# Last expert pair's down weights by quarters of output columns, scattered outputs added on VectorE, and a new order in heads and gates

## The reference

```python
  x   = LN(x)
  A   = (rms_norm(HGRN2(q, f, i, state)) * silu(g_o)) @ w_o_a      # 8 heads, 128 x 128 state each
  B   = silu(LN(depthwise_conv31(u_a * sigmoid(u_b)))) @ w_o_b
  mix = (sigmoid(gate_a) * A + sigmoid(gate_b) * B) @ w_out
  x   = LN(alpha * x + mix)
  x   = LN(alpha * x + MoE(x))   # 16 experts in 4 groups: best group, then top-2 in it
```

## Time and profile before

| what | us |
|---|---|
| median of 3 runs (lowest, highest) | 912.35 (911.97, 913.24) |
| the profiled execution: its own time | 911.96 |
| the profiled execution: its span | 910.1 |
| PE busy in the span | 848.2 |
| DVE busy in the span | 397.4 |

### The profile page before, as it was taken

The page is one execution under the profiler, slowest core; times in us unless marked ns, Lnnn a source line. Parts: engine busy times, 40 slices in busy tenths (PEclk is TensorE's granted clock), DMA queues, the critical chain, the costliest instruction groups (busy, mean ns, idle before and its releaser), DMA issues.

```text
span 910.1 us, 12810 instructions
## 1 busy us (share of the span) xinstructions
PE 848.2 (93%) x4904; PEld 532.4 (58%) x4904; DVE 397.4 (44%) x720; ACT 227.5 (25%) x358; POOL 108.1 (12%) x173
## 2 busy tenths in 40 slices
PE   4999999999999999999999999999999899898983
PEld 3989888898989866546554353535435244252330
DVE  6787788879999823215310313103031040310205
ACT  6566666653356131003010011000100001000001
POOL 1366667620000000000000000000000000000000
PEclk9999999999999999998999999999999999999997
DMA  8222222524436523905499999999999999999951
GB/s 302 71 79 80 78 78 85 188 80 154 171 104 237 212 107 153 372 0 208 163 429 428 428 428 428 426 428 427 429 427 429 428 428 428 428 428 428 427 255 59
DMA packets 30420, 248.95 MB, mean 274 GB/s; under 512 B 4462, under 2 KB 7918, under 8 KB 17962
## 3 DMA queue, kind: packets, MB, share of 16 engines
q1 hardware_dynamic: 27840, 247.07, 66.2%
q10 hardware_dynamic: 2538, 1.32, 0.5%
HBM read 245.89 MB, written 2.48 MB: 273 GB/s over the span
## 4 chain that ended last, share of the span: by engine, by line
PE 53%; DVE 19%; DMA 15%; POOL 5%; issue 4%; ACT 3%; POOLq 0%; DVEq 0%; ACTq 0%; SPq 0%
PE ps L437 52%; DMA ring<-in_w_up_e 8%; DMA ring<-in_w_gate_e 7%; DVE ar L1503 6%; DVE split_t L1511 3%; POOL ring L1240 2%; DVE ring L1390 1%; DVE ring L1403 1%; POOL ring L1226 1%; PE ps L772 1%; DVE split_w L1349 1%; POOL ar L1255 0%; DVE mid L1521 0%; POOL ar L1253 0%; DVE split_w L1354 0%
## 5 line engine op out<-in xcount | busy, mean ns | idle before, releaser
L437 PE MATMUL ps<-ring,ar 128*64 128x512 f32 (+1 forms) x1120 | 268.2, 594 | 10.6 <-DMA ring<-in_w_gate_e 3.9
L437 PEld LDWEIGHTS ps<-ring,ar 128*64 128x64 f32 (+1 forms) x1120 | 99.1, 140 | 168.5 <-issue 152.6
L437 PE MATMUL ps<-ring,xT 128*64 128x512 f32 (+2 forms) x896 | 161.4, 458 | 7.0 <-DMA ring<-in_w_gate_e 6.7
L437 PEld LDWEIGHTS ps<-ring,xT 128*64 128x64 f32 (+1 forms) x896 | 84.3, 152 | 79.0 <-issue 63.8
L1720 DVE TENSOR_TENSOR ar<-ar,ps 128x512 f32<-128x512 f32 (+1 forms) x42 | 28.7, 684 | 224.4 <-PE ps L437 224.4
L437 PE MATMUL ps<-split_x,split_t 128*128 128x320 f32 x672 | 101.7, 313 | 4.7 <-DVE split_t L1511 4.1
L437 PEld LDWEIGHTS ps<-split_x,split_t 128*128 128x128 f32 x672 | 100.1, 191 | 6.0 <-issue 3.8
L437 PE MATMUL ps<-split_x,split_w 128*128 128x320 f32 x480 | 80.4, 324 | 6.6 <-DVE split_w L1354 2.7
L437 PEld LDWEIGHTS ps<-split_x,split_w 128*128 128x128 f32 x480 | 73.8, 195 | 11.1 <-issue 2.5
L437 PE MATMUL ps<-ar 128*64 128x64 f32 (+6 forms) x304 | 74.1, 375 | 3.1 <-ACT ar L1174 1.2
L1503 DVE SCALAR_TENSOR_TENSOR ar<-ar,params 128x350 f32<-128x350 f32 x116 | 67.7, 584 | 4.1
(11 more groups left out here) (190 smaller groups left out, 721.8 us busy)
## 6 DMA issues: line engine op xcount, KB each, us to landing
ring<-in_w_gate_e SPq DMA_DIRECT2D x32, 2048.0 KB, 27.5
ring<-in_w_up_e SPq DMA_DIRECT2D x32, 2048.0 KB, 25.9
ring<-in_w_down_e SPq DMA_DIRECT2D x32, 2048.0 KB, 31.7
ring<-in_w_in SPq DMA_DIRECT2D x56, 512.0 KB, 4.3
ring<-in_w_o_a SPq DMA_DIRECT2D x8, 512.0 KB, 5.9
ring<-in_w_out SPq DMA_DIRECT2D x1, 4096.0 KB, 14.6
ring<-in_w_o_b SPq DMA_DIRECT2D x4, 512.0 KB, 5.1
ar<-in_x_prompt SPq DMA_DIRECT2D x2, 512.0 KB, 4.5
```

What stands on the lines that cost most here:

```text
L437: return pe.matmul(out, lhsT, rhs, start=start, stop=stop)
```

## The change

It does these things:

- **Heads.** DVE does the masks of the previous head before the decay of the current one and takes the first addition of the fold over all three tiles (`level_fold`); POOL keeps three additions and waits for `fold_ready`. PE does `levels` before `prev_kT`, and `cur_q` before `prev_states`; `prev_out` waits for all sums at its start. ACT moves `prev_states` behind `key_exp`, and `prev_cross`, `q_copy`, `prev_sa` ahead of `level_exp`. The split of the first convolution weight (`u_high(0, 0)`, `u_low(0, 0)`) moves into the middle of the last turn. The first turn with a previous head keeps its PE order.
- **Gates.** `t_high`, `t_low`, `out_gates` and `gates` go by single matrices (q = 0, 1) where they went by two, and the taps are dealt out in threes and fours behind each. The number of taps is the same.
- **Router.** The transposes of tile 0 move between the second and third tile of `w_out`; `logits(1)` comes before the transposes of tile 2; the `keep_busy` counts are 0, 6 and 1 where they were 2, 8 and 2. `picks` and `gate_picks` are one wide instruction each. `gather` signals after each half, and the first two gate groups wait for the first half alone.
- **End.** The last pair's down weights are laid out on the host by quarters of output columns (`w_down_end`, same size, same rows of 16 KB for a partition); each quarter is 16 matmuls of 256 columns, copied, scattered (3 matmuls) and added to `yacc` on DVE while the next quarter runs. `sums_back` is gone. Statistics and normalisation read `yacc` from SBUF and write `y_out` (in `ring`); the `value_load` comes after them.

```diff
         wring = ring[:, :, :, :, :].rearrange("p g b k n -> p (g b k n)").rearrange("p (g m k n) -> p g m k n", g=SLOTS, m=2, k=2)
...
+                sp.wait_ge(e["group_used"], 2 * PARTS * end_i + g - SLOTS + 1)
+                if g < 2 * PARTS - 4:
+                    load_group(end_i, g)
+                else:
+                    sp.dma_start(wslot[:, g % SLOTS, :], column(a["w_down_end"], g % 4)).then_inc(group_in[g % SLOTS], 16)
...
+                if first_prev:
+                    prev_kT(*prev, True)
+                    levels(*prev, True)
+                    prev_states(*prev)
                 if pprev:
                     rms(*pprev)
-                if prev:
-                    prev_kT(*prev, first_prev)
-                    levels(*prev, first_prev)
+                    levels(*prev, False)
+                    prev_kT(*prev, False)
+                    cur_q(*cur, False, True)
                     prev_states(*prev)
-                if pprev:
-                    cur_q(*cur, False, True)
...
+            levels(3, 1, False)
             prev_kT(3, 1, False)
-            levels(3, 1, False)
-            prev_states(3, 1)
             pe.wait_ge(h["rstd_ready"], 7)
             conv_gate(0)
+            prev_states(3, 1)
...
+                if t == 1:
+                    to_features(x1, x1_ready, x1T_done, x1T_sb, X1_BANKS, 0, 1)
...
-            to_features(x1, x1_ready, x1T_done, x1T_sb, X1_BANKS, 0, 2)
-            keep_busy(2)
+            to_features(x1, x1_ready, x1T_done, x1T_sb, X1_BANKS, 1, 2)
             logits(0)
+            logits(1)
             to_features(x1, x1_ready, x1T_done, x1T_sb, X1_BANKS, 2, 3)
-            logits(1)
             logits(2)
-            keep_busy(8)
+            keep_busy(6)
...
-            keep_busy(2)
+            keep_busy(1)
...
-                last.then_inc(e["eXT_done"], 1)
+                    if k % 4 == 3:
+                        last.then_inc(e["eXT_done"], 1)
 
             def gate(n, i, b):
-                pe.wait_ge(e["eXT_a"], n + 1)
-                pe.wait_ge(e["eXT_b"], n + 1)
                 for g in range(PARTS * b, PARTS * b + 4):
+                    if g % PARTS == 0:
+                        pe.wait_ge(e["eXT_a"], n + 1)
+                    if g % PARTS == 2:
+                        pe.wait_ge(e["eXT_b"], n + 1)
                     group(g, i)
...
+            def last_down(i, b, c):
+
+                g = PARTS * b + 8 + c
+                group(g, i)
+                if c >= 2:
+                    pe.wait_ge(e["eos_ready"], PAIRS + c - 2)
+                w = wslot[:, g % SLOTS, :].rearrange("p (m k n) -> p m k n", m=2, k=KT)
+                for k in range(KT):
+                    for m in range(2):
+                        last = mm(ps[64 * m:64 * m + 64, 6 + c % 2, 0:QN], ehT[:, k, 64 * m:64 * m + 64], w[:, m, k, :], k == 0, k == KT - 1)
+                last.then_inc(e["group_used"], 1)
+
+            def last_scatter(c):
+
+                pe.wait_ge(e["eos_ready"], PAIRS + c)
+                if c >= 2:
+                    pe.wait_ge(e["y_added"], 6 * (PAIRS - 1) + 3 * c - 3)
+                for t, (_, n) in enumerate(TILES):
+                    mm(ps[0:n, 3 * (c % 2) + t, 0:QN], eGT[:, t, 0:n], eos[:, c * QN:c * QN + QN], True, True).then_inc(e["y_done"], 1)
...
+                    last_down(i, b, 0)
+                    last_down(i, b, 1)
                     pe.wait_ge(e["eGT_sb"], n + 1)
                     pe.wait_ge(e["y_added"], 6 * n)
-                    sums_back()
-                down(n, i, b)
+                    last_scatter(0)
+                    last_down(i, b, 2)
+                    last_scatter(1)
+                    last_down(i, b, 3)
+                    last_scatter(2)
+                    last_scatter(3)
...
-                    act.wait_ge(t_done, 2 * n - 2)
-                for q in range(2):
-                    signal(act, act.activation(t_hi[1 - b][q][1], stl[:, b, 8 * q:8 * q + 8].rearrange("p k n -> p (k n)"), ACT.Copy), thi_ready, 2 * n + q + 1)
+                    act.wait_ge(t_done, 2 * n - 3 + q)
+                signal(act, act.activation(t_hi[1 - b][q][1], stl[:, b, 8 * q:8 * q + 8].rearrange("p k n -> p (k n)"), ACT.Copy), thi_ready, 2 * n + q + 1)
...
+            def last_copy(c):
+                act.wait_ge(e["group_used"], PARTS * (PAIRS - 1) + 9 + c)
+                signal(act, act.activation(eos[:, c * QN:c * QN + QN], ps[:, 6 + c % 2, 0:QN], ACT.Copy), e["eos_ready"], PAIRS + c)
...
+                pool.wait_ge(h["fold_ready"], n + 1)
...
-                pc(pool.tensor_tensor(am[:, :, 0:3 * BLK], am[:, :, 0:3 * BLK], am[:, :, 4 * BLK:LW], ALU.add))
...
-                signal(pool, pool.tensor_tensor(hAS[0:BLK, 2, 0:BLK], am[:, 0:BLK], am[:, BLK:2 * BLK], ALU.add), h["as_ready"], 2 * n + 2)
+                pc(pool.tensor_tensor(hAM[:, :, 0:2 * BLK], hAM[:, :, 0:2 * BLK], hAM[:, :, 2 * BLK:4 * BLK], ALU.add))
+                signal(pool, pool.tensor_tensor(hAS[BLK:P, 0:2, BLK:P], hAM[BLK:P, 0:2, 0:BLK], hAM[BLK:P, 0:2, BLK:2 * BLK], ALU.add), h["as_ready"], 2 * n + 1)
+                signal(pool, pool.tensor_tensor(hAS[0:BLK, :, 0:BLK], hAM[0:BLK, :, 0:BLK], hAM[0:BLK, :, BLK:2 * BLK], ALU.add), h["as_ready"], 2 * n + 2)
...
+            def level_fold(i, b):
+                n = 2 * i + b
+                signal(dve, dve.tensor_tensor(hAM[:, :, 0:3 * BLK], hAM[:, :, 0:3 * BLK], hAM[:, :, 4 * BLK:LW], ALU.add), h["fold_ready"], n + 1)
...
-                level_decay(*cur)
                 if prev:
                     level_mask(*prev, first_prev)
                     last_mask(*prev, first_prev)
+                    level_fold(*prev)
+                level_decay(*cur)
                 if pprev:
                     pprev_out(*pprev)
                 if nxt:
                     w_low(*nxt, 0)
+                else:
+                    u_low(0, 0)
                 if prev:
                     prev_final(*prev, first_prev)
                 if first:
                     w_low(*nxt, 1)
                 query_side(*cur)
+                carry_side(*cur, first)
                 if nxt is None:
-                    u_low(0)
+                    u_low(0, 1)
                 elif not first:
                     w_low(*nxt, 1)
-                carry_side(*cur, first)
...
+            def taps(first, last):
+
+                for c in range(CT):
+                    if max(first, c * TAPS) < min(last, c * TAPS + TAPS):
+                        conv_taps(c, max(first - c * TAPS, 0), min(last - c * TAPS, TAPS))
...
-            conv_taps(0, 20, 29)
+            t_low(0, 0)
+            t_low(0, 1)
+            taps(16, 22)
             conv_gate(3)
-            t_low(1)
-            conv_taps(0, 29, 31)
-            conv_taps(1, 0, 3)
+            t_low(1, 0)
...
-                t_low(p)
-                out_gate(2 * p - 4)
-                out_gate(2 * p - 3)
-                conv_taps(1, 6 * p - 9, 6 * p - 3)
...
-            conv_taps(3, 0, 8)
-            t_low(11)
-            conv_taps(3, 8, 31)
+                for q in range(2):
+                    t_low(p, q)
+                    out_gate(2 * p - 4 + q)
+                    taps(6 * p + 14 + 3 * q, 6 * p + 17 + 3 * q)
+            for p in range(6, NG):
+                for q in range(2):
...
             dve.wait_ge(pos_done, 1)
-            step(dve.tensor_copy(rt[:, 0], ps[:, 0, 0:3 * NE].rearrange("p (t n) -> p t n", t=3)))
...
+                pk(dve.tensor_copy(cur, rt[:, 0:3:2, :, bass.ds(2 * p, 2)]))
+                signal(dve, dve.tensor_tensor(pm4, slots_wide, slot_of(cur[:, 0]), ALU.is_equal), e["pick_ready"], n + 1)
...
+                signal(dve, dve.tensor_tensor(gm4, pm4, slot_of(cur[:, 1]), ALU.mult), e["gpick_ready"], n + 1)
...
+            def last_add(c, t):
+                n, j = TILES[t][1], 6 * (PAIRS - 1) + 3 * c + t + 1
+                dve.wait_ge(e["y_done"], j)
+                yv = yacc[0:n, t, c * QN:c * QN + QN]
+                signal(dve, dve.tensor_tensor(yv, yv, ps[0:n, 3 * (c % 2) + t, 0:QN], ALU.add), e["y_added"], j)
...
+            def norm2(t, ch, round_done):
+                n = TILES[t][1]
+                norm_gain(y_out[0:n, t, :], yacc[0:n, t, :], t, n, g2[0:n, :], ch)
+                norm_offset(y_out[0:n, t, :], t, n, b2[0:n, :], rstd2, y_ready, 3 * round_done)
+
+            for c in range(2):
+                for t in range(3):
+                    last_add(c, t)
+            for t in range(3):
+                half2(t, 0, step)
+            for t in range(3):
+                last_add(2, t)
+            for t in range(3):
+                last_add(3, t)
+                half2(t, 1, step)
+                mean2(t, 0)
+            for t in range(3):
+                norm2(t, step, 0)
             more = dve.value_load(flag[0:1, :], min_val=0, max_val=1)
             with dve.If(more != 0):
...
```

(1 more changed line is left out.)

320 lines of the change are left out of this document (146 added, 174 removed).

## The result

The changed kernel takes 904.12 us (median of 4 runs, 902.0 to 905.52) against 912.8 us of the kernel before beside it; the ratio is 0.9904 with a 95% interval of 0.9881 to 0.9926. On another chip, in five rounds, it was 902.26 us (901.28 to 903.86) against 912.98, ratio 0.9889 (0.9872 to 0.9906). So it is faster by 9 to 11 us, not by the 15.8 that were forecast, and 904.12 lies above the range.

What follows compares the result with a forecast made beforehand. The prediction took a fixed-length weight stream to bound the kernel, leaving only front and tail to gain: 911.96 - 8.3 (front) - 7.4 (tail) = 896.3 us profiled, plus 0.39 for the median, 896.6 us; range 892.5 to 901.5.

Steps and rivals of the forecast that it cites:

- Heads, 6.2 us: Attention head turns: PE's waits vanish, five turns take 96.3 instead of 101.63 us, plus 0.9 before them; gain 6.2 us.
- 18.95 us, still 0.3 below PE: Head turn: DVE's 18.25 us plus 0.7 for the added addition stays under PE's own 19.26 us.
- the 96.3 of the sum: Heads: five turns at PE's own 19.26 us each, against 101.63 us before.
- turns stay at 20.1: Heads rival: DVE, with more work, is held up by POOL's instructions; 4.2 us back, 900.8 us; chance 0.12.
- Convolution start, another 0.6: DVE's convolution start comes 0.6 us earlier beyond the heads' gain, as the states now stand behind PE's first projection.
- DVE's waits in the convolution, 1.0: Convolution: splits follow closely behind ACT, costing DVE 1 us of waits, so DVE finishes 5.9 us earlier.
- PE idle about 6 us and -2.1 for the low clock: Before the convolution's mean: PE idles about 6 us, then restarts at a low clock, losing 2.1 us.
- Router 4.5: Router to gather: earlier transposes and logits, fewer filling matmuls, wide picks, a half-gather signal; gain 4.5 us.
- the rival: Low clock lasts into the gather and first gate matmuls: 3 us lost, 899.6 us; chance 0.10.
- Stream moves whole: Expert weight transfers: the same 88 transfers, starting 8.3 us earlier and moving as a whole.
- Tail 7.4: End of the last pair: no `sums_back`, quarters, earlier normalisation; gain 7.4 us.
- Quarters slower, the rival by the Trainium skill: Last down quarters: 128 exposed weight loads cost 6.8 us, giving 903.1 us; quarters rival's chance 0.05.

Runs made afterwards that it cites:

- no_sums: `warm_mean` with POOL's three level sums cut to 2 columns each (incomplete computation); time of 2849.1 us not usable, first convolution product at 146.57 us instead of 153.07.
- no_fold: `warm_mean` with DVE's first level sum cut to 2 of 192 columns per tile (incomplete computation); 896.75 us.
- warm_act: Changed kernel with seven unused matmuls in PE's pause before the mean and ACT's two copies of the second convolution weight moved behind the square; 899.83 us.
- old_gates: Changed kernel with the earlier order of gates and convolution taps on DVE and ACT; 900.14 us.
- the second: Second trace of the unaltered changed kernel, from its repeat on another chip; 902.26 us.
- warm_mean: Changed kernel with ten unused matmuls in PE's pause before the convolution's mean; 900.26 us.
- tail_only: Kernel before with only the new end of the last pair; heads, gates and router as before; 906.74 us.

## Why the prediction was wrong

By its steps, in the prediction's order:

- **Heads, 6.2 us: this is the step that failed.** 0.7 of it came in the first turn (39.79 to 39.05 from the common zero; predicted 0.9). The five turns gave 2.65 instead of 5.3. The error stands in "18.95 us, still 0.3 below PE": DVE's work in a turn is 19.5, above PE's 19.26, and another 0.3 of waiting for ACT makes the 19.8 that the turns take. The addition was priced rightly. What was put at nothing is what DVE's instructions cost in their new place: 0.76 us more in the decay (4.16 for 3.40), because POOL's sums now fall into it, and 0.34 more in the query side (3.93 for 3.59). Against them stand 0.28 less in the last product of `carry_side` and 0.24 less in the two splits. `no_sums` shows the decay's part directly, and `no_fold` that DVE is the bound: with the 0.76 us of the addition gone, five turns take the 96.3 of the sum. The query side's part stays open; more of it runs beside POOL's products than before, but no run separates that. The rival "turns stay at 20.1" named this mechanism and was given only 0.12.
- **Convolution start, another 0.6: wrong sign.** The first product gained 0.9 less than the turns had, by the 1.75 us wait behind ACT's copies, which the prediction had not looked for; `warm_act`, without it, has the product 1.9 earlier.
- **DVE's waits in the convolution, 1.0:** 1.3 (a gain of 2.46 at the first product, 1.12 at the last tap), and DVE's waits for ACT there are 1.0 and 0.4 us. Together with the above the mean moved by 1.4, not 5.9.
- **PE idle about 6 us and -2.1 for the low clock:** 6.18 and -2.0 (4.54 for 2.52). Right as a difference: PE was to be 12 us early and DVE 5.9, and they were 7.8 and 1.1, since the lost heads' gain is missing from both. `old_gates` shows that the part of the change that made the pause gained nothing for it.
- **Router 4.5:** 3.9 by marks in the first trace, 5.1 in the second. In the first trace and in `warm_mean` a low clock fell into the gather too; the rival gave 3 us for it, and the gather takes 1.0 longer.
- **Stream moves whole:** right, no hole.
- **Tail 7.4:** 5.4 from the released transfer to the first normalising instruction, 5.6 to the end. The missing 2.0 us are four small ones: the first quarter starts 0.3 later relative to `up` (0.83 us wait for ACT's copy), `up` itself ends 0.3 later relative to the stream; PE needs 20.6 instead of 19.6, since changing between quarters and scatters costs about 0.25 us each time; DVE has 3.36 us behind PE's end instead of 3.0, with additions of 0.42 instead of 0.3. The first two are not of the new end itself: in `tail_only` the first quarter waits 0.48 us and starts 0.6 earlier by the stream.
- **Quarters slower, the rival by the Trainium skill** ("TensorE: Matmul & The Clock Gate", Part 3, "What overlaps and what doesn't"): 64 instructions of 256 columns take 7.13 us, 111 ns each against 109 for half of the old 218. So the trace shows no exposed weight loads, and the rival's 6.8 us did not come. (Its 903.1 was also 0.4 low, as it left out the 0.39 between the profiled execution and the median.) On this form of matmul the page's rule does not hold here.

The sum by measured steps: 3.37 at the stream and 5.55 behind it are 8.9 us between the two profiled executions, counted from the common zero; their spans differ by 7.6, as the changed one reached that zero 1.3 later. Not settled is how much of the executions' own spread (902.0 to 905.52 in one session) is start and how much is clock.

## What to carry to other kernels

When an order is changed, price not only the instruction that is added but the neighbours that it makes run side by side: what GpSimd did beside them made seven small float32 subtractions of VectorE 23% longer (4.16 us for 3.40), and up to 49% with one sum more (5.05), and together with the added sum that was enough to turn the engine with 0.3 us to spare into the bound. Making an engine finish early that then waits for another gains nothing and can cost the clock. Find a mark early in the trace from which to count, before two traces are compared to a microsecond.

## What the hardware showed that was not expected

- The same seven DVE subtractions took 2.96 us with POOL's sums cut, 3.40 beside POOL's own seven subtractions in the kernel before, up to 4.16 with three sums on POOL falling into them, and 4.72 to 5.05 with four.
- Executions of kernels that are alike so far reach the same row up to 2.2 us apart (35.76 to 37.95), and six of them then keep step within 0.1 us for 153 us (153.06 to 153.15).
- Twenty matmul instructions without use in a pause of 6.2 us gave 2 us back; two more filling matmuls behind the logits, where the clock is already low, and one more behind the counts went with a stream 2.4 us later, 1.5 of it waiting for them.
